# Hybrid attention and pooling layer on one core: the first weight columns on a second queue, and the warm-up matmuls fed by another engine

## What is computed

```python
hn   = RMSNorm_pre(x)
proj = hn @ W_in            # -> [q | k | v | gate_a | u_pool | gate_b], 1024 columns each
y_a  = StickBreakingAttn(q, k, v) * silu(gate_a)     # 8 heads x 128
y_b  = MultiScalePool(u_pool) * silu(gate_b)         # 4 groups x 256, windows 2/4/8/16
x    = x + RMSNorm_post(concat(y_a, y_b) @ W_out)
```

## Time and profile before

| | |
|---|---|
| Median of 3 runs | 717.91 us (717.52 to 718.13) |
| Profiled execution, its own time | 717.29 us |
| Its span, first to last instruction | 715.6 us |
| TensorE busy | 706.4 us (99% of the span) |
| VectorE, ScalarE, GpSimd busy | 82%, 61%, 10% |
| First warm-up matmul starts | 1.85 us |
| First matmul of step 0 starts | 6.43 us |

### The profile page before, as it was taken

How to read it: one execution, slowest core, us unless ns; L and a number is a source line. 1 busy time by engine, 2 the same in 40 slices (tenths; PEclk the granted TensorE clock), 3 DMA queues, 4 the chain that set the end, 5 groups by cost and what they waited for, 6 DMA issues and landing times.

```text
span 715.6 us, 9846 instructions
## 1 busy us (share of the span) xinstructions
PE 706.4 (99%) x3724; PEld 609.5 (85%) x3724; DVE 584.0 (82%) x749; ACT 434.7 (61%) x577; POOL 73.3 (10%) x94
## 2 busy tenths in 40 slices
PE   8999999999999999999999999999999999999995
PEld 7888888888888888888888888888888888888884
DVE  3499977988798888898897978898888984376787
ACT  5765576566776656767766677756688434253561
POOL 0000000210020110011110011020001000001001
PEclk9999999999999999999999999999999999999998
DMA  8965446567746666655766666656655307468985
GB/s 299 390 192 142 125 115 163 164 173 196 179 119 173 171 177 170 176 147 150 199 136 175 180 163 166 169 138 175 180 173 177 118 13 251 118 167 230 282 320 236
DMA packets 38544, 128.59 MB, mean 180 GB/s; under 512 B 4321, under 2 KB 5345, under 8 KB 37601
## 3 DMA queue, kind: packets, MB, share of 16 engines
q1 hardware_dynamic: 31440, 102.78, 42.3%
q0 software_dynamic: 6912, 25.17, 21.1%
q10 hardware_dynamic: 144, 0.01, 0.0%
HBM read 123.74 MB, written 4.19 MB: 179 GB/s over the span
## 4 chain that ended last, share of the span: by engine, by line
PE 96%; DVE 2%; issue 0%; POOL 0%; DVEq 0%; ACT 0%; ACTq 0%
PE ps L1895 36%; PE ps L1903 19%; PE ps L1839 11%; PE ps L1806 9%; PE ps L1807 9%; PE ps L1805 9%; DVE mix L1697 1%; PE ps L1940 1%; PE ps L1938 1%; PE ps L1871 1%; DVE mix L1599 0%; PE ps L1822 0%; PE ps L1830 0%; PE ps L1832 0%; DVE mix L1627 0%
## 5 line engine op out<-in xcount | busy, mean ns | idle before, releaser
L1895 PE MATMUL ps<-a_ops,w_hi 128*128 128x512 f32 x1120 | 270.8, 391 | 0.0
L1895 PEld LDWEIGHTS ps<-a_ops,w_hi 128*128 128x128 f32 x1120 | 205.1, 188 | 39.5
L667 ACT ACTIVATE w_hi<-raw 128x1024 fp32r<-128x1024 f32 x155 | 163.6, 1056 | 69.4 <-PE ps L1895 40.2
L1121 DVE TENSOR_TENSOR raw_lo<-raw,w_hi 128x1024 fp32r<-128x1024 f32 x155 | 188.8, 1224 | 19.4 <-ACT w_hi L667 18.5
L1903 PEld LDWEIGHTS ps<-a_ops,raw_lo 128*128 128x128 f32 x1120 | 145.7, 191 | 6.4
L1903 PE MATMUL ps<-a_ops,raw_lo 128*128 128x256 f32 x1120 | 149.9, 283 | 0.0
L1752 POOL DMA_DIRECT2D raw<-w_heads x40 | 35.0, 875 | 316.6 <-DMA raw<-w_heads 231.7
L1805 PE MATMUL ps<-w_hi,a_ops 128*128 128x512 f32 x160 | 62.3, 390 | 0.0
L1807 PE MATMUL ps<-w_hi,a_ops 128*128 128x512 f32 x160 | 62.3, 389 | 0.0
L1806 PE MATMUL ps<-raw_lo,a_ops 128*128 128x512 f32 x136 | 53.0, 389 | 0.0
L1136 DVE TENSOR_TENSOR raw<-raw 128x1024 f32<-128x1024 f32 x40 | 48.6, 1215 | 1.2 <-PE ps L1807 1.2
(11 more groups left out here) (228 smaller groups left out, 1025.9 us busy)
## 6 DMA issues: line engine op xcount, KB each, us to landing
raw<-w_heads SPq DMA_DIRECT2D x100, 512.0 KB, 4.4
raw<-w_heads POOLq DMA_DIRECT2D x40, 512.0 KB, 5.9
raw<-w_out SPq DMA_DIRECT2D x35, 512.0 KB, 4.9
raw<-w_v SPq DMA_DIRECT2D x15, 512.0 KB, 10.2
x_rows<-x SPq DMA_DIRECT2D x6, 1024.0 KB, 11.5
mix<-xT SPq DMA_DIRECT2D x16, 256.0 KB, 10.1
out<-mix SPq DMA_DIRECT2D x8, 512.0 KB, 2.7
raw_more<-w_out SPq DMA_DIRECT2D x6, 512.0 KB, 6.8
```

Of the source, the lines that this page charges most:

```text
L667: act.activation(hi_slot(g), raw_slot(raw, slot), ACT.Copy).then_inc(w_hi_done, 1)
L1121: dve.tensor_tensor(raw_slot(raw_lo, slot), raw_slot(raw, slot), hi_slot(g).bitcast(F32), ALU.subtract).then_inc(w_split, 1)
L1895: mm = pe.matmul(dst, hi[:, k * P:(k + 1) * P], a_ops[:, a:a + SEQ], start=k == 0 and p in (0, 1, 5), stop=stop and k == KH - 1, skip_grou ...
```

## The change

Three things change.

1. The first 16 columns (`AHEAD = 16`, 64 bytes for each partition) of each half of the first weights are loaded by ScalarE's queue, as its first two instructions, ahead of `pre_gain_col`. SyncE loads the other 496 columns. The two ScalarE copies now wait for 32, that is for both loads.
2. VectorE makes `fill` and `neg_ones` as its first two instructions, and a semaphore of its own, `ones_ready`, releases TensorE. GpSimd keeps `positions` and `neg_tri`.
3. The warm-up matmuls use `neg_ones` for both operands instead of `neg_tri` and `neg_ones`, and there are 9 instead of 10.

```diff
-WARM = 10
+WARM = 9
+AHEAD = 16
...
-        POOL_CONSTS = 4
+        POOL_CONSTS = 2
...
             load_x(0)
             for g in range(2):
-                sp.dma_start(raw[:, g * BANK:(g + 1) * BANK],
-                             w_v[g * KK][:, 0:BANK]).then_inc(w0_loaded[g], 16)
+                sp.dma_start(raw[:, g * BANK + AHEAD:(g + 1) * BANK],
+                             w_v[g * KK][:, AHEAD:BANK]).then_inc(w0_loaded[g], 16)
...
         def _(act):
+            for g in range(2):
+                act.dma_start(raw[:, g * BANK:g * BANK + AHEAD],
+                              w_v[g * KK][:, 0:AHEAD]).then_inc(w0_loaded[g], 16)
             act.dma_start(pre_gain_col[:, :], pre_gain).then_inc(gain_loaded, 16)
...
-            act.wait_ge(w0_loaded[0], 16)
+            act.wait_ge(w0_loaded[0], 32)
...
-            act.wait_ge(w0_loaded[1], 16)
+            act.wait_ge(w0_loaded[1], 32)
...
         def _(dve):
+            dve.memset(fill[:, :], -1.0).then_inc(filled, 1)
+            dve.wait_ge(filled, 1)
+            dve.tensor_copy(neg_ones[:, :], fill[:, :]).then_inc(ones_ready, 1)
             dve.memset(neg_half[:, :], -0.5).then_inc(vec_const, 1)
...
-            pool.memset(fill[:, :], -1.0).then_inc(pool_const, 1)
-            pool.wait_ge(pool_const, 2)
-            pool.tensor_copy(neg_ones[:, :], fill[:, :]).then_inc(pool_const, 1)
+            pool.wait_ge(filled, 1)
             pool.affine_select(out=neg_tri[:, :], in_=fill[:, :], compare_op=ALU.is_ge, fill=0.0, base=0,
...
-            pe.wait_ge(pool_const, POOL_CONSTS)
+            pe.wait_ge(ones_ready, 1)
             for _ in range(WARM):
-                pe.matmul(bank(V_BANK[1][TT - 1]).rearrange("p (a b) -> p a b", a=TT), neg_tri[:, :],
+                pe.matmul(bank(V_BANK[1][TT - 1]).rearrange("p (a b) -> p a b", a=TT), neg_ones[:, :],
```

More of the change, by code:

```diff
@@ L304, in hybrid_layer @@
         pool_const = sem("pool_const")
+        filled = sem("filled")
+        ones_ready = sem("ones_ready")
         vec_const = sem("vec_const")
```

## The result

| | before | after |
|---|---|---|
| Median of 6 runs | 718.01 us (717.52 to 718.62) | 721.66 us (720.58 to 722.88) |
| Ratio | | 1.0052, 95% interval 1.0042 to 1.0063 |
| Profiled execution: own time, span | 717.29, 715.6 us | 722.88, 721.1 us |
| Mean granted clock of the span | 0.996 | 0.993 |
| First warm-up matmul | 1.85 us | 1.39 us |

The change makes the kernel 0.52% slower, 3.7 us. The forecast was 717.8 us, with 716.9 to 718.8 as its range. The profiled execution of after is the slowest of its six, so its trace shows more than the median.

The account below looks back on a forecast made before the run. TensorE was taken as the bound, busy 706.4 of 715.6 us. Step 0's fifth matmul moving from 7.87 to 7.77 gave 717.29 - 0.10 = 717.2 profiled; from the median 717.91, 717.8 us was predicted, range 716.9 to 718.8.

Parts of the forecast that it names:

- the gain behind the strips: ScalarE's queue: pre_gain_col, behind two 16-column weight loads, lands at 4.9 instead of 3.7, just hidden by the weights.
- the late gain: Rival, ScalarE's start: pre_gain_col lands after 5.57 and delays step 0, up to +0.83 us, 718.7; chance 0.15.
- the point of decision (5.57): Landing time of pre_gain_col beyond which step 0's fifth matmul slips, each further microsecond costing one.
- three times the one transfer without overlap: Upper end for pre_gain_col's landing: all three ScalarE loads take the one's time from issue, about 6.4.
- The late clock: Rival, TensorE idle 1.1 us before step 0: clock rises later, up to +2.0 us, 719.9; chance 0.13.
- The constants on VectorE: Start of VectorE: both constants take 0.40 us, so TensorE starts at about 1.3 to 1.4, 0.5 us earlier.
- the forecast of -0.1 us: Step 0's fifth matmul, first on weight half 1, starts at 7.77 instead of 7.87, 0.10 us earlier.
- the 6.7 of the sum: TensorE's clock rises to the high level at 6.7 instead of about 7.2, through the earlier warm-up start.
- a wash: Two 16-column loads cost 0.2 us of all sixteen engines against 3% fewer bytes per SyncE load, leaving weight landing unchanged.
- The earlier weights: Rival, first weight loads: 16-column reads of w_v make both halves land sooner, at best -1.02 us, 716.9; chance 0.26.
- Faster, same, slower: Chances for the whole kernel against a 1.44 us threshold (716.47 to 719.35): faster 0.04, same 0.89, slower 0.07.

Follow-up runs that it names:

- SyncE held: Kernel after the change, with SyncE's loads from step 1 on waiting until pre_gain_col has landed: 720.78 us, one run.
- weights first: Kernel before, with SyncE loading the two weight halves ahead of x of step 0: 721.8 us, one run.
- gain on SyncE: Kernel after, with pre_gain_col as SyncE's first load, 16-column loads leading ScalarE's queue, 12 warm-up matmuls: 718.38 us, ratio 1.0013.
- one strip: Kernel after, with only half 0's 16-column load on ScalarE's queue, half 1 loaded whole by SyncE: 719.38 us, ratio 1.0023.
- other loads ahead: Kernel after, the two 16-column weight loads replaced by two unused 8 KB loads of pre_gain, SyncE loading all 512 columns: 721.92 us, one run.
- other loads, 24 matmuls: Kernel after, two unused 8 KB pre_gain loads replacing the 16-column weight loads, and 24 warm-up matmuls: 719.59 us, one run.
- 24 matmuls: Kernel after the change with 24 warm-up matmuls instead of 9: 719.69 us, ratio 1.0028.
- strips only: Kernel before plus the two 16-column weight loads ahead of pre_gain_col, constants on GpSimd and ten warm-up matmuls kept: 721.58 us, ratio 1.0052.
- gain-first version: Kernel after, with pre_gain_col as ScalarE's first load and the two 16-column weight loads behind it, nine warm-up matmuls: 719.43 us, ratio 1.0027.
- version without strips: Kernel after without the 16-column weight loads, SyncE loading all 512 columns; constants on VectorE, nine warm-up matmuls: 717.59 us, ratio 1.0005.

## Why the prediction was wrong

**The step that failed** is "the gain behind the strips". I put the landing of `pre_gain_col` at 4.9, with 6.4 as the upper end; it landed at 8.8. The middle came from the earlier trace rows: 46 packets of ScalarE's queue in 0.2 us, so 288 in 1.25. That rate was read while SyncE's queue was carrying x at 40 packets in the same 0.2 us, and the two numbers belong together: when SyncE's queue slows down, ScalarE's slows with it. The packets show why a small load gains nothing. In the version with SyncE held, three loads of 248 or 256 KB and three of 8 KB, each queue had moved 432 packets when the gain landed, 144 for each load whatever its size (first two lines, 0 to 6.95 us). The queues take turns by packets, not by bytes.

```profile
q1 hardware_dynamic: 432, 0.77, 47.7%
q10 hardware_dynamic: 432, 0.02, 4.1%
...
q1 hardware_dynamic: 543, 0.99, 50.6%
q10 hardware_dynamic: 428, 0.02, 3.9%
...
q1 hardware_dynamic: 248, 0.48, 92.2%
q10 hardware_dynamic: 4, 0.00, 0.1%
```

So the n-th load of ScalarE's queue has to wait for about as long as the n-th of SyncE's. It landed 0.2 us behind it, once 0.5, in all rows but the last three, the versions that have two strips ahead of the gain and SyncE's later loads running:

| kernel | place | SyncE's load landed | ScalarE's landed |
|---|---|---|---|
| before | 1 | x, 3.5 | gain, 3.7 |
| weights first | 1 | half 0, 5.8 | gain, 6.0 |
| gain on SyncE | 1 | gain, 2.6 | strip 0, 2.8 |
| gain on SyncE | 2 | x, 4.3 | strip 1, 4.5 |
| one strip | 2 | half 0, 5.6 | gain, 5.8 |
| other loads ahead | 3 | half 1, 7.1 | gain, 7.3 |
| other loads, 24 matmuls | 3 | half 1, 7.3 | gain, 7.8 |
| SyncE held | 3 | half 1, 6.7 | gain, 6.9 |
| 24 matmuls | 3 | half 1, 7.1 | gain, 8.2 |
| strips only | 3 | half 1, 7.3 | gain, 8.3 |
| full change | 3 | half 1, 7.0 | gain, 8.8 |

(Landing is issue plus "us to landing". Where a strip and its bulk add to one semaphore, the trace can't say which of the two landed first; of the rows above this touches the one for the single strip and half 1 of the last four.) In the last three rows the gain came 1.0 to 1.8 us behind half 1. The other four lines above are the full change, 0 to 7 and 7 to 9 us: 428 of ScalarE's 432 packets had moved by 7.0, and the last four came singly over the next 1.6 us, beside 248 packets of SyncE's later loads. Holding those loads took this tail away. Why so few packets wait so long, and why the two versions with other loads have less of it, is open. The forecast could have been made from the earlier trace rows and the timeline alone, by pairing the places: the gain in third place lands no sooner than SyncE's third load, at 7.1. That gives `x_hi` at 7.1, step 0 at 8.5, and +1.5 us before any clock.

The Trainium skill (DMA: Bandwidth & Descriptors, the section on queues, rings and completion order) says that each DMA engine goes round-robin between the queues it has work for. The trace agrees: 432 packets on each queue in the same time. I knew the two queues to be served side by side and still priced a full queue by a rate, not by its partner's progress.

**The rival that came true** is the late gain, with its chance of 0.15 and its upper end at +0.83 us. The mechanism and its place were right, the point of decision (5.57) too; the size was cut off by the wrong upper end, "three times the one transfer without overlap", which is no bound when the other queue slows down.

**The late clock** came with it, and its chance of 0.13 was taken as apart from the late gain, though an idle TensorE is what both need. I had priced it as a rise that comes late. In the full change and the gain-first version it was a fall. The clock was up at 4.9 in the one (0.40 us for the ninth warm-up matmul) and at 6.9 in the other (four weight loads in 0.76 us), and at 0.50 by 8.4 and by 9. In the weights-first version no fall is recorded and the matmuls are 0.43 us apart from 8.85 to 13.7; there the rise did come late. Together the two rivals were worth about 2.1 + 1.7 us.

**The sum's other terms.** The constants on VectorE took 0.17 and 0.23 us (0.40 forecast), and TensorE started at 1.39 (1.35). The version without strips measured no difference, as the forecast of -0.1 us said, and its fifth matmul waits for half 1, at 7.63 (7.77 forecast). Its clock was high by 6.19 (four weight loads in 0.76 us), earlier than the 6.7 of the sum; since half 1 sets the fifth matmul, this gave nothing. The strips' own cost I called a wash, by 0.10 us of engine time each. Behind the gain they make both halves ready 0.4 us later, 0.3 us at the fifth matmul, so that was wrong as well: a strip is ready only with its place in the queue, and the copy waits for it. The Trainium skill's warning against small transfers (DMA: Bandwidth & Descriptors, the rules for kernel authors) gave the better direction than my row of engine time, though not by its reason: what the strips cost was not engine time but their turn.

**The earlier weights** did not come. The rows of `w_v` had been touched by the strips when the bulk arrived, and it took 4.7 us all the same. Why a 256 KB load of `w_v` takes 5.0 us as the first load, where one of x takes 2.7 to 3.0, is open.

**Faster, same, slower.** The forecast gave 0.07 to slower. It rested on rows that bounded the gain from above wrongly. With the pairing the middle would have been 717.9 + 1.5 = 719.4, at the border to slower that the prediction set (719.35), before any clock.

## What to carry to other kernels

A small load did not travel at its own speed here but in its place: count how many transfers stand ahead of it in its own queue, and look up when the transfer of the same place in the other queue lands. That is the earliest time for it where both have as many packets, as the loads compared here (144 each). Put the load that the first computation waits for first, however small the ones that could go ahead of it seem. And when a change moves the start of the work, fill TensorE's wait up to it, and no further: here the idle stretch cost nearly as much again as the wait, and a warm-up that ended 1 us after the weights were ready gave 0.5 us away.

## What the runs showed of the hardware that I had not expected

- An 8 KB load landed 1.8 to 7.1 us after its issue, by what stood ahead of it and what the other queue carried. A load of 8 KB and one of 256 KB, both of 128 rows, are 144 packets each.
- The clock, once high, fell back during the start. In the full change it fell at 8.2 to 8.4 us, with TensorE idle since 5.3. TensorE had been idle from 5.5 to 6.9 and from 8.0 to 8.2 us in the gain-first version; the granted clock is 0.67 for 8 to 10 us and 0.50 for 10 to 12, and its runs spread from 717.9 to 721.6 us. With 16 warm-up matmuls the same kernel is at 718.25 us.
- The column of the granted clock reads 1.00 in the first 6 us of every trace, also where matmuls of 512 columns are 0.43 us apart. In the weights-first version it stays at 1.00 through 8.85 to 13.7 us, where they are 0.43 us apart too. So 1.00 at the start doesn't prove the high level; until the column has shown a change the spacing has to be read.
